# Order of the front stage of a two-layer hybrid block: head norms split in two steps, evictions ahead of roundings, gate rows from a repeated stationary column, squares in four groups

## The reference, cut to what matters

```python
h = rmsnorm(x, g_mix); proj = h @ w_in
# forgetting attention: 8 heads of 64
q = rmsnorm(q, q_gain); k = rmsnorm(k, k_gain)
cum_f = cumsum(log_sigmoid(f_logit + b_f))
s = q @ k.T * scale + cum_f[i] - cum_f[j]      # causal, then softmax, @ v
# short convolution
y_sc = sb * causal_dwconv(sc * sv)
# gated delta rule: 4 heads of 128
dn_qkv = silu(causal_dwconv(dn_qkv))
o = gated_delta_rule(l2norm(q), l2norm(k), v, g, beta)
```

## The kernel before

| n | unit | what becomes of the result |
|---|---|---|
| 0 to 4, 6 | fox query, key, value | ScalarE copies to `fqkv` (banks 0 to 3) |
| 5, 7, 8, 9, 10, 11 | dn (delta rule q, k, v) | ScalarE copies to `conv` (line 980), VectorE runs 8 tap operations (lines 1464, 1466: "taps") |
| 12, 17 | z | ScalarE Silu |
| 13, 14, 15 and 16, 18, 19 | short convolution: c, v, b | ScalarE copy; VectorE product (line 1441) and 6 tap operations; VectorE product |
| 20 on | gates, branch projections | ScalarE Sigmoid; VectorE merge |

## Time and profile before

### The profile page before, as it was taken

How to read it: one execution, slowest core, us unless ns; L and a number is a source line. 1 busy time by engine, 2 the same in 40 slices (tenths; PEclk the granted TensorE clock), 3 DMA queues, 4 the chain that set the end, 5 groups by cost and what they waited for, 6 DMA issues and landing times.

```text
span 1127.7 us, 17514 instructions
## 1 busy us (share of the span) xinstructions
PE 1100.3 (98%) x7442; PEld 973.8 (86%) x7442; DVE 767.3 (68%) x937; ACT 556.2 (49%) x664; POOL 36.4 (3%) x98
## 2 busy tenths in 40 slices
PE   9989999999999999999998999999999999999997
PEld 8888998997989999998797888888888888888886
DVE  5486788554668998787677575556667866656555
ACT  6466564333535443445665454444455665444443
POOL 6000000000000000000003200000000000000000
PEclk9998999999999999999999999999999999999999
DMA  8542443333355555554453355555534435555551
GB/s 306 181 156 75 150 150 116 111 116 110 130 175 194 187 187 187 187 187 167 169 180 134 129 174 190 194 196 198 191 119 174 153 115 187 184 190 187 187 187 56
DMA packets 27455, 185.07 MB, mean 164 GB/s; under 512 B 3169, under 2 KB 3681, under 8 KB 5618
## 3 DMA queue, kind: packets, MB, share of 16 engines
q1 hardware_dynamic: 26208, 182.46, 45.9%
q10 hardware_dynamic: 1170, 1.49, 0.4%
HBM read 182.89 MB, written 1.05 MB: 163 GB/s over the span
## 4 chain that ended last, share of the span: by engine, by line
PE 89%; DVE 7%; ACT 2%; issue 1%; POOL 0%; DVEq 0%; ACTq 0%; POOLq 0%
PE ps L2041 12%; PE ps L2056 12%; PE ps L2043 12%; PE ps L1971 10%; PE ps L2009 9%; PE ps L2015 9%; PE ps L2010 9%; PE ps L1977 5%; DVE low L1299 2%; DVE arena L1466 1%; PE ps L2073 1%; PE ps L1991 1%; PE ps L2375 1%; PE ps L2237 1%; PE ps L2143 0%
## 5 line engine op out<-in xcount | busy, mean ns | idle before, releaser
L891 ACT ACTIVATE whi<-raw 128x2048 fp32r<-128x2048 f32 x170 | 324.3, 1913 | 333.1 <-PE ps L2056 165.8
L1299 DVE TENSOR_TENSOR low<-raw,whi 128x2048 fp32r<-128x2048 f32 x170 | 389.2, 2293 | 40.3 <-ACT whi L891 37.4
L2009 PE MATMUL ps<-hboth,whi 128*128 128x256 f32 x880 | 221.0, 289 | 3.3 <-ACT conv L980 3.3
L2010 PE MATMUL ps<-hboth,whi 128*128 128x256 f32 x880 | 217.0, 284 | 0.0
L2009 PEld LDWEIGHTS ps<-hboth,whi 128*128 128x128 f32 x880 | 169.4, 192 | 7.9 <-ACT whi L891 3.6
L2010 PEld LDWEIGHTS ps<-hboth,whi 128*128 128x128 f32 x880 | 169.7, 193 | 0.7 <-issue 0.2
L2041 PE MATMUL ps<-whi,ahi 128*128 128x512 f32 x416 | 164.2, 395 | 2.8 <-issue 1.9
L2043 PE MATMUL ps<-whi,alo 128*128 128x512 f32 x416 | 162.8, 391 | 0.0
L1971 PE MATMUL ps<-hboth,whi 128*128 128x512 f32 x512 | 128.1, 392 | 0.0
L2015 PE MATMUL ps<-hboth,low 128*128 128x256 f32 x880 | 124.2, 284 | 0.5 <-DVE low L1299 0.5
L2056 PE MATMUL ps<-low,ahi 128*128 128x512 f32 x416 | 119.7, 389 | 0.0
(11 more groups left out here) (376 smaller groups left out, 1216.1 us busy)
## 6 DMA issues: line engine op xcount, KB each, us to landing
raw<-in_ffn_up SPq DMA_DIRECT2D x32, 1024.0 KB, 4.8
raw<-in_ffn_down SPq DMA_DIRECT2D x32, 1024.0 KB, 4.9
raw<-in_w_up SPq DMA_DIRECT2D x22, 1024.0 KB, 4.9
raw<-in_w_gate SPq DMA_DIRECT2D x12, 1024.0 KB, 4.9
raw<-in_w_down SPq DMA_DIRECT2D x11, 1024.0 KB, 4.9
raw<-in_w_dn SPq DMA_DIRECT2D x6, 1024.0 KB, 4.9
raw<-in_w_sc SPq DMA_DIRECT2D x6, 1024.0 KB, 4.8
raw<-in_w_branch SPq DMA_DIRECT2D x6, 1024.0 KB, 4.8
```

Source lines behind the costliest of these rows:

```text
L891: act.activation(whi[:, u % SPLIT, :], raw[:, u % RAW, :], ACT.Copy).then_inc(sem("hi_done"), 1)
L1299: dve.tensor_tensor(wlo[:, u % RAW, :], raw[:, u % RAW, :], whi[:, u % SPLIT, :].bitcast(F32), ALU.subtract).then_inc(sem("lo_done"), 1)
L2009: pe.matmul(out, wh, hi[:, k0 + k, :], start=opens and k == 0, stop=False, skip_group_check=True)
L2010: pe.matmul(out, wh, lo[:, k0 + k, :], start=False, stop=False, skip_group_check=True)
```

## The change

Six edits, all in the first layer's front:
1. `fox_norm` becomes two steps: `fox_sums` (squares, sums per head) at key 17 and `fox_norm` (root, reciprocal, products) at key 20.
2. What follows a unit other than a branch projection is put into the order at once, behind its second half and ahead of the steps at key 2n+1, no longer held until behind the next first half.
3. `fcum` and its two VectorE operations go. `fox_cum` multiplies instead, per head, a stationary matrix that repeats one column of the log gates 128 times by the triangle (or by `before`, the triangle less one): 8 products of 128 columns.
4. `fox_cum(t)` waits for the copies of its own 128 tokens, not for all four.
5. `dn_square` is four steps of 4 products at keys 25, 26, 27, 28; the first two wait for the first square alone. `dn_cum` moves to 27, `dn_unit` and `att_scores(0, 0)` to 28.
6. GpSimd makes `before`, one operation of 128 x 128.

```diff
-        18: [("fox_norm",)],
+        17: [("fox_sums",)],
+        20: [("fox_norm",)],
         22: [("fox_turn", 0)],
         24: [("fox_turn", 1), ("fox_cum", 0), ("dn_silu",)],
-        26: [("fox_cum", 1), ("dn_square",), ("dn_cum",), ("dn_unit",)],
-        27: [("att_scores", 0, 0)],
+        25: [("dn_square", 0)],
+        26: [("fox_cum", 1), ("dn_square", 1)],
+        27: [("dn_square", 2), ("dn_cum",)],
+        28: [("dn_square", 3), ("dn_unit",), ("att_scores", 0, 0)],
         29: [("att_norm", 0, 0)],
...
         else:
-            held.extend(then)
+            order.extend(then)
...
+            then(pool.tensor_scalar(before[:, :], tri[:, :], -1.0, None, ALU.add))
             made["front"] = n[0]
...
-                for t in range(TT):
-                    dve.scalar_tensor_tensor(out=fcum[:, t], in0=wide(tri[:, :].unsqueeze(1), [FH, P]),
-                                             scalar=-1.0 if t == 0 else 0.0,
-                                             in1=wide(zz[:, 3, t, 0:FH].unsqueeze(2), [FH, P]), op0=ALU.add, op1=ALU.mult)\
-                       .then_inc(sem("fox_f"), 1)
...
             def fox_cum(t):
-                pe.wait_ge(sem("fox_f"), TT)
-                pe.wait_ge(sem("fox_T"), 4)
+                pe.wait_ge(sem("small_lsg"), 1)
+                pe.wait_ge(sem("fox_T"), 2 * t + 2)
                 for b in range(2):
-                    out = by(ps[:, 2 * t + b, :], 4)
-                    pe.matmul(out, ones[:, :], fcum[:, t, 4 * b:4 * b + 4, :], start=True, stop=True)\
-                      .then_inc(sem("fox_cummed"), 1)
+                    for h in range(4):
+                        ins = pe.matmul(ps[:, 2 * t + b, h * P:(h + 1) * P],
+                                        zz[:, 3, t, 4 * b + h:4 * b + h + 1].to_broadcast([P, P]),
+                                        before[:, :] if t == 0 else tri[:, :], start=True, stop=True)
+                    ins.then_inc(sem("fox_cummed"), 1)
...
-            def dn_square():
-                pe.wait_ge(sem("dn_sq"), 2)
-                for i in range(16):
+            def dn_square(j):
+                pe.wait_ge(sem("dn_sq"), j // 2 + 1)
+                for i in range(4 * j, 4 * j + 4):
                     ins = pe.matmul(ps[:, 7, i:i + 1], dsq[:, P * i:P * (i + 1)], ones[:, 0:1], start=True, stop=True)
-                ins.then_inc(sem("pe_single"), 1)
+                ins.then_inc(sem("dn_squared"), 1)
```

More of the change, by code:

```diff
@@ L585, in build @@
         tri64 = sb("tri64", [P, P])
+        before = sb("before", [P, P])
         blk64 = sb("blk64", [P, P])
@@ L640, in build @@
         PT2 = view(16384, 1024).rearrange("p (b n) -> p b n", b=2)
-        fcum = view(15360, 2048).rearrange("p (t h j) -> p t h j", t=TT, h=FH)
         fbias = xs[:, :, :].rearrange("p t n -> p (t n)").rearrange("p (h j) -> p h j", h=FH)
@@ L771, in build @@
         made = {}
-        single = [s[0] for s in order if s[0] in ("dn_square", "dn_cum", "pool_mm")]
+        single = [s[0] for s in order if s[0] in ("dn_cum", "pool_mm")]
         single = {name: 1 + at for at, name in enumerate(single)}
@@ L1230, in final, with fox_sums @@
                    .then_inc(sem("final_act"), 1)
-            def fox_norm():
+            def fox_sums():
                 for g, v in fox_taken:
@@ L1235, in fox_norm @@
                 act.activation(xs[:, :, 0:2 * FW], fqkv[:, :, 0:2 * FW], ACT.Square).then_inc(sem("fox_sq"), 1)
+            def fox_norm():
                 root(ss[:, :, :], 1.0 / FD)
@@ L1248, in dn_unit @@
             def dn_unit():
-                act.wait_ge(sem("pe_single"), single["dn_square"])
+                act.wait_ge(sem("dn_squared"), 4)
                 act.activation(dnr[:, 1], ps[:, 7, 8:16].rearrange("p (h t) -> p h t", t=TT), ACT.Sqrt, bias=eps[:, :])\
@@ L1263, in _ @@
                          gla_arg=gla_arg, gla_v=gla_v, gla_mask=gla_mask,
-                         gla_g=gla_g, gla_sum=gla_sum, gla_turn=gla_turn, final=final, fox_norm=fox_norm,
+                         gla_g=gla_g, gla_sum=gla_sum, gla_turn=gla_turn, final=final, fox_sums=fox_sums, fox_norm=fox_norm,
                          dn_silu=dn_silu, dn_unit=dn_unit, dn_sum=dn_sum, ab_sum=ab_sum, ab_turn=ab_turn)
@@ L1302, in _, with root @@
             roots = [0]
-            def root(ap, ins=None):
+            def root(ap):
                 roots[0] += 1
-                if ins is not None:
-                    ins.then_inc(sem("root_in"), 1)
                 dve.wait_ge(sem("root_out"), roots[0])
@@ L1488, in dn, with fox_sums @@
                 taps("dn_conv", 4, 3 * BT, 2 * e, j, dnT[:, 2 * e:2 * e + 2, :])
+            def fox_sums():
+                dve.wait_ge(sem("fox_sq"), 1)
+                sq = xs[:, :, 0:2 * FW].rearrange("p t (h d) -> p t h d", d=FD)
+                dve.tensor_reduce(ss[:, :, :], sq, AX.X, ALU.add).then_inc(sem("root_in"), 1)
             def fox_norm():
-                dve.wait_ge(sem("fox_sq"), 1)
                 nh = 2 * FH
                 qk = fqkv[:, :, 0:2 * FW].rearrange("p t (h d) -> p t h d", d=FD)
-                sq = xs[:, :, 0:2 * FW].rearrange("p t (h d) -> p t h d", d=FD)
-                root(ss[:, :, :], dve.tensor_reduce(ss[:, :, :], sq, AX.X, ALU.add))
+                root(ss[:, :, :])
                 for t in range(TT):
@@ L1553, in dn_unit @@
             def dn_unit():
-                dve.wait_ge(sem("pe_single"), single["dn_square"])
+                dve.wait_ge(sem("dn_squared"), 4)
                 root(dnr[:, 1])
@@ L1898, in _ @@
                          pool_u=pool_u, gla_low=gla_low, gla_qk=gla_qk,
-                         params=params, small_turn=small_turn, sc=sc, dn=dn, fox_norm=fox_norm,
+                         params=params, small_turn=small_turn, sc=sc, dn=dn, fox_sums=fox_sums, fox_norm=fox_norm,
                          dn_sum=dn_sum, ab_sum=ab_sum, ab_turn=ab_turn, gla_sum=gla_sum, gla_turn=gla_turn,
```

## The result

The changed kernel takes 1149.77 us (median of 4 runs, 1148.51 to 1152.26) against 1131.56 us (4 runs, 1129.44 to 1133.86): ratio 1.0179, 95% interval 1.0159 to 1.0199 (the two medians alone give 1.0161), slower by 18 to 20 us. The forecast was 1139.6 us with a range of 1133.5 to 1143.0: right in sign, wrong in size by more than its range allowed. The profiled execution took 1148.51 us, its span grew by 19.1 us from 1127.7.

The account below looks back on a forecast made before the run. TensorE, busy nearly all the span, was taken as the bound, with the 60 to 105 us chain of waits through VectorE. 1.3 + 2.0 + 3.2 + 1.7 = +8.2 on 1131.4 gave 1139.6 us, range 1133.5 to 1143.0.

Parts of the forecast that it names:

- VectorE's walk: VectorE's queue, 58 to 97 us: unit 7's taps 59.0, gate chain 62.4, remainder 10 at 68.7, last taps' end 96.0.
- the Silu's start: The three Silu start when VectorE's last taps end, 96.0 against 96.70 before; first square ready at 99.9.
- The waits: TensorE's waits: 1.0 us for remainder 11, 3.9 head product, 4.0 first square, 1.2 `dn_unit`, 2.0 and 3.2 attention.
- key 25: TensorE stands 4.0 us before `dn_square(0)`, from 96.0 to 99.9, for the first square.
- key 29: `att_norm(0, 0)` stands behind unit 14's product and taps on VectorE; TensorE waits 2.0 us for it.
- `fox_cum` itself: The 32 new records of 128 columns take 3.8 us as before: 0; bounds nothing gained and +1.2.
- From key 39 on evictions are ScalarE's alone: From key 39 on, evictions delay a rounding by 0.5 us, hidden by two units of lead: 0, at most 0.5.
- the clock: After TensorE's 4.0 us wait and thin squares, one low-clock stretch of 3.4 us: +1.7; bounds 0 and +3.4.
- The rival with more low clock: A long low stretch, or a second around pauses at keys 27 and 28: 1141.3 or 1143 us; chance 0.12.
- Nothing: Eviction order doesn't matter and all waits trade even: within 0.2% of 1131.4 us; chance 0.05.
- no attention stalls: VectorE's order at keys 29 and 37 is not as read, -5.2: 1134.4 us; chance 0.07.
- faster rival: VectorE's queue, 58 to 96 us: last taps end by 88.2, waits and low clock go: 1128.9 us; chance 0.11.

Follow-up runs that it names:

- experiment 9: The changed kernel with 12 unread products of 128 columns ahead of each of TensorE's waits at keys 22 and 25: 1148.11 us, ratio 1.0167.
- experiment 7: The kernel before with edit 1 alone, the head norm split into two steps at keys 17 and 20: 1131.86 us, ratio 1.0031.
- Experiment 4: The kernel before with evictions put ahead (edit 2) only from unit 20 on: 1138.47 us, ratio 1.0076.
- experiment 1: The changed kernel with evictions ahead only up to unit 19, held again from unit 20 on: 1142.05 us, ratio 1.0116.
- experiment 2: The changed kernel with edit 2 undone, all evictions held: 1136.54 us, ratio 1.0067.
- Experiment 10: The changed kernel with only ScalarE's dn copies ahead, sums and norm at keys 18 and 19, all squares at 27, scores at 28: 1124.11 us, ratio 0.9953.
- experiment 3: The kernel before with edit 2 alone: 1146.76 us, ratio 1.0159.
- experiment 6: The changed kernel with edit 5 undone, all squares, `dn_cum` and `dn_unit` at key 26, first scores at 27: 1147.73 us, ratio 1.0168.
- experiment 5: The kernel before with edit 5 alone, the squares in four groups from key 25 on: 1135.45 us, ratio 1.0061.
- experiment 8: The kernel before with edits 3, 4 and 6 alone, the gate rows: 1130.66 us, ratio 1.0016.
- experiment 11: As Experiment 10, but with two groups of squares at key 26 and two at key 27: 1125.59 us, ratio 0.9976 against the kernel before.

## Why the prediction was right and wrong

**VectorE's walk held, the Silu's start did not.** Its timeline in the changed kernel:

```profile
59.21 0.62 DVE L1463 TENSOR_SCALAR arena<-conv,colp 128x256 f32<-128x256 f32 x2 [1.17 <-ACT conv L984]
...
62.61 0.19 DVE L1415 TENSOR_TENSOR zz<-ps,rowp 128x32 f32<-128x32 f32 x1
...
69.26 2.29 DVE L1305 TENSOR_TENSOR low<-raw,whi 128x2048 fp32r<-128x2048 f32 x1 [2.42 <-ACT whi L895]
...
83.05 2.36 DVE L1499 TENSOR_TENSOR arena<-arena,ss 128x1024 f32<-128x1024 f32 x2
...
93.79 2.72 DVE L1465 SCALAR_TENSOR_TENSOR arena<-conv,colp,arena 128x256 f32<-128x256 f32 x6
```

Forecast: taps 59.0, gate chain 62.4, remainder of unit 10 at 68.7, last taps' end 96.0; here 59.21, 62.61, 69.26 and 96.5. The 2.42 us of idle time before 69.26 are the operations of edit 3, which bought nothing, as said. But the prediction let the Silu start with the last taps' end, at 96.0, and they started at 97.95. ScalarE had copied out `fox_cum(0)` until 96.64 and then loaded a table for 1.28 us; that copy waited for TensorE, late by the low clock from 82.3 on. In experiment 9, where that stretch was not low, the Silu started at 96.43, right behind VectorE's taps.

**The waits held.** Those at the remainder, key 22, key 25, `dn_unit`, key 29 and key 37 were forecast at 1.0, 3.9, 4.0, 1.2, 2.0 and 3.2, together 15.3 us, and measured 1.27, 3.70, 3.03, 1.52, 0.90 and 3.35, together 13.8. Key 29 was over-sized by more than half. At key 25 TensorE itself arrived late, held up by the low clock from 82.3 on, while the squares came 2 us late with the Silu.

**`fox_cum` itself: 0, right.** 1.70 us a step for 1.72 (experiment 7). That is 106 ns a record. The page of the Trainium skill that the prediction weighed, "TensorE: Matmul & The Clock Gate", section "Back-to-back issue gap", gives about 81 ns for a weight load with its 128-column product. By that figure, as an estimate, a step of 16 records would take 1.3 us; the trace has 1.70.

**The step that failed first: "From key 39 on evictions are ScalarE's alone; they delay a rounding by 0.5, hidden by two units of lead: 0, at most 0.5".** What stands in the same keys as those evictions was not read. At key 65 the eviction delays no rounding but the delta rule's sums, and costs a wait 3.6 us longer and the low clock behind it. Going from the product before that wait (272.22 before, 284.36 after) to the product at 288.5 us of before, the shift grows from 12.1 to 20.2: 8.0 us. Experiment 4 made it appear alone (8.1 at this place, +9.1 in all); experiment 1 took the wait away and left 3.0 of low clock here (-7.7 in all).

**The second: the clock, "I take one of 3.4: +1.7".** The forecast gave 3.3 us back for the stretch at 105 and charged 1.7, net -1.6. Measured: 10.8 less 4.4 = +6.4. Five stretches followed instead of one, the first four behind or around waits that the walk had found and the fifth behind key 65's. The prediction charged every wait its own length and only one of them a clock. Its reason, "Both thin stretches of before ended in the low clock", also left one out: 77.3 to 80.7 was as thin (1.18 us busy) and stayed high before, and in experiment 4 the same products were followed by 3.4 us of low clock. A thin stretch may bring the clock down; these traces don't say when. The rival with more low clock went the right way, but 1143 was its limit.

**The ledger.** 8.2 forecast, 8.0 more for the clock, 3.6 for the wait at key 65, 1.5 less for the other waits: 18.3, against 19.1 between the spans. Most of the last 0.8 us lies near 617 us of before: the low stretch there is counted as 1.5 us given back, but the shift falls only by 0.8 across it.

**The rivals.** "Nothing" and "no attention stalls" fall: experiment 2 shows the stalls at keys 29 and 37 to be edit 2's. The faster rival named its place rightly, the gate chain held up by the taps of unit 7. Experiment 10 took the taps out of the gate chain's way and came out 5.1 us faster than before. It also held every other eviction, moved the squares two keys later and put the sums and the norm at 18 and 19, so no single one of these is shown to have made it. The rival's waits of 3.3 and 1.0 us went, which fits the shift of -4.4. Its other terms didn't come: the last taps end at 94.8, not 88.2, and 6.8 us of low clock stayed.

**What stays open.** What sets the length of a low stretch, and whether one comes at all. In the five traces with the wait of 4.5 us at key 65, 10.2 us followed (the changed kernel, experiments 3 and 4) or 13.7 (6 and 9). In the eight without it (the kernel before, experiments 1, 2, 5, 7, 8, 10 and 11), none followed, but for 6.8 in experiment 1. The changed kernel and experiment 1 have one program up to unit 20, yet their low stretches at 82 to 108 us last 6.8 and 3.4 us in one and 3.4 and 6.8 in the other. The one near 617 us is there in the kernel before and in experiments 4, 8 and 11 and in none of the others. So losses and gains of the clock can be shown in each trace, but the totals of two kernels that differ in the front differ by a few microseconds that no reading of the edit would give.

## What to carry to other kernels

Where all engines walk through one order, moving one kind of step moves it past everything else that has the same place: list for every key what it now precedes, on each engine, down to the last key, and ask of each whether its input is ready earlier than that of the moved step. A step that must wait for a whole unit doesn't belong ahead of one whose input is there; here one such place made 8.0 of 19.1 us. Move only the instruction that frees the scarce buffer (the copy), not the work that hangs on it (the taps); experiment 10 did so, with other moves beside it.

A wait of TensorE should be charged with more than its length when it is a few microseconds long: at key 65 the wait cost 3.6 us more than before and the low clock behind it 4.4 (43% of 10.20). That price is not certain: the wait of 2.2 us near 77.5 cost no clock before and 3.4 us of low clock in experiment 4.

## What the runs showed of the hardware that was not expected

The granted clock stayed low for 3.4, 6.8, 10.2 or 13.7 us at a time, the end of the kernel aside. In experiment 4 it fell behind 3.4 us without a single product and stayed low for 10.2 us in which TensorE was busy for 9.99. In experiment 1 it fell behind 3.4 us with 2.54 busy and stayed for 6.8, busy throughout. Being busy, then, didn't bring it back at once. In the changed kernel more than half of 290.5 to 300.7 are the delta rule's small products (64 rows, until 296.3) and the rest full ones; no run separates the two.

One program doesn't have one clock. The kernel before, on the chip of experiments 4, 5 and 7, took 1127.4 to 1127.7 us at a mean granted clock of 0.997 or 0.998 in five of 17 executions, and 1129.0 to 1131.6 at 0.991 to 0.995 in the other twelve. So a difference of 2 or 3 us between two single traces can be the clock's alone.

Repeating one column 128 times as the stationary matrix costs nothing beside an ordinary one. Records of the repeated column start 0.11 us apart in the changed kernel (16 in 1.70 us), and so do the 32 records near 7 us that have ordinary stationary matrices.
